# Sums over gathered expert rows: four experts of 32 tokens in column groups in place of one expert of 128 tokens under a diagonal

## The chip, the cores and the metric

The kernel runs on one core of one Trainium2 chip. The metric is the device time of one execution in microseconds (us), the median of several runs.

## The reference

Two transformer blocks run one after the other on 512 tokens of width 1024. The part that the change touches is the last layer of the second block, a retrieval layer over 16384 experts:

```python
query = (ht @ w_query).reshape(t, PEER_HEADS, 2, PEER_HALF)
sub_scores = einsum('thpd,hpkd->thpk', query, sub_keys)
half_vals, half_idx = top_k(sub_scores, 16)
cand = half_vals[:, :, 0, :, None] + half_vals[:, :, 1, None, :]
top_vals, top_pos = top_k(cand, 16)
experts = i1 * 128 + i2                      # from half_idx and top_pos
gates = softmax(top_vals)
u = expert_down[eb]
act = gelu(einsum('td,thkd->thk', xb, u)) * gb
vv = expert_up[eb]
return einsum('thk,thkd->td', act, vv)
```

Each token has 8 heads with 16 experts each; each expert has a down row and an up row of 1024 float32. All arithmetic is in float32.

## The kernel before, in words

There are four tiles of 128 tokens (`TT` = 4, t) and eight heads (`H` = 8), so 32 head steps, n = 8 t + h. Down and up rows lie side by side in one table (`expert_pair_2`), so one indirect DMA fetches for 128 partitions a row of 2048 floats, 1.05 MB. A head step needs 16 of these gathers, and the layer 512. Gather m = 16 n + r brings expert r of each of the 128 tokens, one token to a partition.

The engines run one program each, and meet only at semaphores. For head step n, in eight parts (`PARTS`):

- GpSimd (L822 to L836) waits for the expert numbers (`ids_done`) and for a free buffer (`pair_free`), then issues the gather. There are `PAIRS_0` = 8 buffers during the first eight head steps (`FIRST` = 128 gathers), `PAIRS` = 11 after them (L282 to L303).
- VectorE multiplies the down half with the token row `h2r_2` and sums it (`dot`, L1740 to L1744), two dots to a part, and in parts 2 to 7 does the top-16 selection of head step n + 2 (`topk_part`, L1726); the numbers go to `ids` and the softmax gates to `gate_p` (L1717 to L1724).
- ScalarE (`coefs`, L1207 to L1219) applies Gelu to the dots, multiplies each by its gate (L1214), and writes one 128 x 128 diagonal matrix for each gather, `ident` scaled by the coefficient (L1219). In the first eight head steps it does this for four gathers at a time, later for two.
- TensorE (`up_sums`, L2286 to L2292) multiplies each diagonal with the up half of its buffer, two matmuls of 512 columns in two PSUM banks, and then frees the buffer. A float32 matmul shows as two records in the profile, so a gather has four records on L2290. `edge` (L2302) opens and closes the sums with zero matmuls; `peer_scores` (L2277) makes the scores for the selection.
- After the last head of a tile, `last_norm` (VectorE L1752, ScalarE L1240) adds the result to `xr` and normalizes it; SyncE stores it (L713). It is placed after head step 6 of the next tile.

Tile 0's eight head steps are not alone. The attention of tiles 1 to 3, its output projection and the query projections are cut into 67 steps (`attend(s)`), and a planner (`PLAN`, L573 to L578) deals them by weight over the eight parts of the first six head steps: stick-breaking attention (steps 6 to 28, head steps 0 and 1), forgetting attention, called fox (29 to 56, head steps 2 and 3: L2117 to L2137), then norms, output projection and query projections (57 to 66, head steps 4 and 5); `query_b` goes on to head step 12. In each part every engine does its share of the layer first, then its share of the planned steps. Each engine keeps this order, so a late engine holds up whatever stands behind it in its own program.

The SyncE queue loads weights in an order written out by hand (L693 to L713); among it the loads of `w_query` for head h (L706), each after the projection before it.

The two earlier matmul shapes that matter below: `modulation` (L1798 to L1806) multiplies one or two columns of `cvec` with four different weight slabs, and writes to PSUM partitions 32 j, j = 0 to 3, in a loop over j inside a loop over c.

## Time and profile before

| | us |
|---|---|
| median of 3 runs | 3261.64 |
| lowest, highest | 3260.54, 3271.85 |
| the profiled execution | 3263.08 |
| its span, first to last instruction | 3261.3 |

The page gives for each engine its busy time and for the span in 40 slices of 81.5 us the busy share in tenths. PE is the matmul side of TensorE and PEld its weight loads, which overlap; DVE is VectorE, ACT ScalarE, POOL GpSimd, SP SyncE. PEclk is the clock that was granted to TensorE, as a share of 2.4 GHz: it has two levels, 1.00 (2.4 GHz) and 0.50 (1.2 GHz), and a value between is a mean over time. The DMA row is the busy share of the 16 DMA engines. "Idle before" in a group of instructions is what the engine waited ahead of them, and the arrow names what ended the wait.

### The profile page before, as it was taken

The numbers are of one execution on the slowest core, as the hardware profiler recorded it, in microseconds if no ns is written. First come the engines' busy times: TensorE is split into PE (matmuls) and PEld (weight loads), VectorE is DVE, ScalarE is ACT, GpSimd is POOL, SyncE is SP. The second block draws the span as 40 slices with busy tenths as digits, with TensorE's granted clock in tenths as the row PEclk, the third lists the DMA queues.
The fourth block names the chain that finished last, engine by engine and source line by source line (L and its number), as shares of the span: only waits on it lengthen the run. The fifth ranks groups of instructions, "written<-read, shape, count | busy, mean of one in ns | idle before, by whom it ended". The sixth has DMA issues, their size and how long they took to land.

```text
span 3261.3 us, 27350 instructions
## 1 busy us (share of the span) xinstructions
PE 2663.6 (82%) x8698; PEld 1292.5 (40%) x8698; DVE 1425.1 (44%) x3362; ACT 872.7 (27%) x2245; POOL 661.9 (20%) x601
## 2 busy tenths in 40 slices
PE   2999999956878777399879999889898777777776
PEld 1444554442332333154466545444443332333322
DVE  1295521140000000400157545655667777777774
ACT  2005420011000000211226534232333333333332
POOL 1001100000000000000002111224335455444552
PEclk8999999968888989699789877999999999999998
DMA  7417814728999999512136745689999999999996
GB/s 248 164 52 241 300 61 143 244 95 321 386 377 380 393 387 384 199 65 67 38 128 226 290 163 224 243 317 369 418 417 421 421 421 421 421 398 421 421 421 278
DMA packets 207351, 928.11 MB, mean 285 GB/s; under 512 B 18809, under 2 KB 58808, under 8 KB 124798
## 3 DMA queue, kind: packets, MB, share of 16 engines
q0 software_dynamic: 80704, 558.26, 42.6%
q1 hardware_dynamic: 116736, 359.68, 30.0%
...
## 4 chain that ended last, share of the span: by engine, by line
PE 38%; DMA 20%; DVE 7%; ACT 6%; issue 4%; ACTq 1%; POOL 1%; DVEq 0%; POOLq 0%; SPq 0%
DMA ring<-in_expert_pair,ids 15%; PE bank L2290 9%; PE bank L1995 9%; PE bank L1789 6%; PE bank L2008 4%; PE bank L1795 3%; DMA arena_v<-in_expert_pair,ids 3%; DVE ring L1744 2%; DMA arena_h<-in_expert_pair,ids 1%; ACTq L1002 1%; PE bank L2118 1%; PE bank L2117 1%; ACT arena_h L1219 1%; POOL ring L835 1%; ACT arena_w L1214 1%
## 5 line engine op out<-in xcount | busy, mean ns | idle before, releaser
L2290 PE MATMUL bank<-ring,arena_h 128*128 128x512 f32 x1772 | 840.9, 624 | 183.0 <-ACT arena_h L1219 182.9
L835 POOL DMA_INDIRECT ring<-in_expert_pair,ids x443 | 519.5, 1173 | 1161.3 <-PE bank L2290 633.0
L2290 PEld LDWEIGHTS bank<-ring,arena_h 128*128 128x128 f32 x1772 | 340.0, 198 | 652.6 <-issue 370.2
L1744 DVE CUSTOM_DVE_ANT_0 ring<-ring 128x1024 f32<-128x1024 f32 x315 | 383.8, 1225 | 177.3 <-DMA ring<-in_expert_pair,ids 158.0
L1789 PE MATMUL bank<-arena_h,ring 128*128 128x512 f32 (+1 forms) x1024 | 373.0, 525 | 15.6 <-DMA ring<-in_w_in 13.5
L1995 PE MATMUL bank<-ring,arena_h 128*64 128x512 f32 x1056 | 292.7, 715 | 65.1 <-ACT arena_h L993 62.0
L1789 PEld LDWEIGHTS bank<-arena_h,ring 128*128 128x128 f32 x1024 | 178.7, 196 | 199.1 <-issue 196.1
L1506 DVE TENSOR_TENSOR arena_q<-arena_q,bank 128x256 f32<-128x256 f32 x32 | 13.5, 421 | 528.5 <-ACT arena_q L996 528.5
L1211 ACT ACTIVATE arena_w<-arena_w 128x2 f32<-128x2 f32 (+1 forms) x224 | 45.4, 203 | 627.1 <-DVE arena_w L1744 626.8
L1995 PEld LDWEIGHTS bank<-ring,arena_h 128*64 128x64 f32 x1056 | 103.4, 163 | 229.9 <-issue 195.8
L1744 DVE CUSTOM_DVE_ANT_0 ring<-ring,arena_w 128x1024 f32<-128x1024 f32 x128 | 153.3, 1223 | 68.5 <-DMA ring<-in_expert_pair,ids 64.4
L1219 ACT ACTIVATE arena_h<-ident,arena_w 128x128 f32<-128x128 f32 x512 | 174.1, 393 | 7.3
L2008 PE MATMUL bank<-ring,arena_q 128*64 128x512 f32 x528 | 120.6, 597 | 21.0 <-DVE arena_q L1509 20.5
...
L1795 PE MATMUL bank<-ring,arena_h 128*128 128x512 f32 x224 | 100.9, 610 | 1.0 <-ACT arena_h L1156 0.8
L1347 DVE SCALAR_TENSOR_TENSOR arena_x<-arena_x,convc 128x512 f32<-128x512 f32 x120 | 90.2, 752 | 4.3
L996 ACT ACTIVATE arena_q<-bank 128x256 f32<-128x256 f32 x32 | 12.3, 384 | 287.6 <-PE bank L1995 287.6
L2290 PE MATMUL bank<-arena_v,arena_h 128*128 128x512 f32 x140 | 70.3, 626 | 21.5 <-ACT arena_h L1219 21.5
L1214 ACT ACTIVATE arena_w<-arena_w 128x1 f32<-128x1 f32 x352 | 81.8, 285 | 5.0
L1795 PE MATMUL bank<-ring,arena_q 128*128 128x512 f32 x176 | 78.9, 609 | 3.6 <-DVE arena_q L1406 3.6
L2290 PE MATMUL bank<-arena_h 128*128 128x512 f32 x136 | 66.8, 614 | 17.5 <-ACT arena_h L1219 17.5
L1211 ACT ACT_TABLE_LOAD x49 | 62.9, 1283 | 48.8 <-DVE arena_w L1744 48.2
...
## 6 DMA issues: line engine op xcount, KB each, us to landing
...
ring<-in_w_exp_down SPq DMA_DIRECT2D x33, 2048.0 KB, 13.8
...
arena_h<-xs_d SPq DMA_DIRECT2D x33, 256.0 KB, 13.8
```

The lines of the kernel that those rows point to most:

```text
L835: pool.indirect_dma_start(pair[pair_of(m)], None, A["expert_pair_2"], bass.IndirectOffsetOnAxis(ap=ids[n % 2][:, r:r + 1], axis=0)).then_i ...
L1002: act.dma_start(ys_d[bass.ds(e * CAP, CAP), 512 * half:512 * half + 512], yblk[b][CAP * half:CAP * half + CAP, :]).then_inc(y_dma[b], 16)
L1211: act.activation(gel[:, r0:r0 + count], dots[:, r0:r0 + count], ACT.Gelu).then_inc(gelu_done, 1)
L1214: act.activation(coef[:, r:r + 1], gel[:, r:r + 1], ACT.Copy, scale=gate_p[n % 3][:, r:r + 1]).then_inc(coef_done, 1)
L1219: act.activation(diag[:, r, :], ident[:, :], ACT.Copy, scale=coef[:, r:r + 1]).then_inc(diag_done, 1)
L1347: link(dve.scalar_tensor_tensor(out=conv[:, cc, :], in0=u_pad[:, cc, k:k + T], scalar=convc[:, cc, k:k + 1], in1=conv[:, cc, :], op0=ALU.m ...
L1744: dve.tensor_tensor_reduce(buf, buf, h2r_2[n // H], 1.0, 0.0, ALU.mult, ALU.add, dots[:, r:r + 1]).then_inc(dots_done, 1)
L1789: mm = pe.matmul(dst, w[:, c, at], rhs[:, c, :], start=(c == 0), stop=(c == chunks - 1))
L1795: mm = pe.matmul(dst, xT[:, c, t * P:(t + 1) * P], w[:, c, at], start=(c == 0), stop=(c == chunks - 1))
L1995: mm = pe.matmul(bank[2 + b][at, :].rearrange("p (g f) -> p g f", g=2), xbT[b][:, c, :], gu[:, :, c, 256 * half:256 * half + 256], start=( ...
L2008: mm = pe.matmul(bank[6 + b][CAP * j:CAP * j + CAP, :], hidT[b][:, k, CAP * half:CAP * half + CAP], slab(n)[:, half, k, 512 * j:512 * j + ...
L2290: mm = pe.matmul(bank[4 + 2 * (n // H % 2) + j][:, :], diag[:, r, :], pair[pair_of(m)][:, D + 512 * j:D + 512 * j + 512], start=False, sto ...
```

## The change

Gather m = 16 n + 4 g + j now brings four experts (4 g to 4 g + 3) of the 32 tokens of block j: partition 32 i + q holds expert 4 g + i of token 32 j + q. Four gathers together bring the same rows as before.

- The dots need token block j repeated in the four partition quarters. Sixteen DMAs within SBUF (`load_h2`) copy the 128 token rows of a tile into four such tiles `h2_q`, 2.1 MB written for each tile, from the SyncE queue: for tile 0 before the first dot, for tile t once all dots of tile t - 1 are done. There is one set of `h2_q`. It lies where the diagonals lay and in the second half of ring slot 5, so there is one gather buffer less: 7, then 10. The buffer order after gather 128 begins with the three that come free (`ORDER`), so GpSimd waits for them at m = 128 and no longer at m = 136.
- The numbers and gates must be laid out the same way. `spread` on TensorE does this with 16 matmuls of 32 columns of `ident` and 12 moving columns, VectorE copies the result (`topk_ids`). The selection moves one part earlier, and `spread` and the copy take part 7.
- `gates_at` on VectorE multiplies a 128 x 32 selecting mask with the 16 gates, once for each head step (128 x 512 elements), and ScalarE scales each 128 x 32 matrix by the Gelu result, four gathers at a time throughout. The product with the gate (L1214) is gone.
- `up_sums` runs for four gathers at a time: for each half of the width four matmuls with 32 stationary columns, one to each column group (PSUM partitions 32 j). The buffers are freed by the last four matmuls.
- `peer_scores(n + 2)` and the sums of the last four gathers of head step n - 1 stand at the start of head step n on TensorE; the attention steps keep their places.

```diff
-PAIRS_0, PAIRS = 8, 11
+PAIRS_0, PAIRS = 7, 10
+Q = 32
...
-        diag = view(arena_h, 2048, K16, P)
+        h2_q = [view(arena_h, 2048, D), view(arena_h, 3072, D), ring[:, 5, 2 * D:3 * D], ring[:, 5, 3 * D:4 * D]]
+        sel_q = view(arena_w, 3092, 2, K16, Q)
+        mask_q = sb("mask_q", [P, Q])
...
-        half_i = small(624, 2, K16)
-        id_f = small(656, K16)
+        picked = small(624, 3, K16)
+        half_i = picked[:, 0:2, :]
+        id_f = small(704, K16)
         gsub, gex = small(672, K16), small(688, K16)
-        gate_p = [small(704 + K16 * i, K16) for i in range(2)] + [sb("gate_c", [P, K16])[:, :]]
-        dots, gel, coef = small(736, K16), small(752, K16), small(768, K16)
+        spread_q = [route(4116, 3, K16), route(4164, 3, K16), small(720, 3, K16)]
+        dots, gel = route(4212, K16), route(4228, K16)
...
+        ORDER = list(range(PAIRS_0, PAIRS)) + [(FIRST + k) % PAIRS_0 for k in range(PAIRS_0)]
 
         def pair_of(m):
 
-            return m % PAIRS_0 if m < FIRST else (m - FIRST) % PAIRS
+            return m % PAIRS_0 if m < FIRST else ORDER[(m - FIRST) % PAIRS]
...
+            def load_h2(t):
+
+                for j in range(P // Q):
+                    for i in range(P // Q):
+                        sp.dma_start(h2_q[j][Q * i:Q * i + Q, :], h2r_2[t][Q * j:Q * j + Q, :]).then_inc(h2_q_in, 16)
+
+            sp.wait_ge(h2_done, TT + 1)
+            sp.wait_ge(q_pe, 4)
+            load_h2(0)
...
+                if h == AHEAD + 2:
+                    sp.wait_ge(h2_done, 2 * TT)
+                    sp.wait_ge(dots_done, FIRST)
+                    load_h2(1)
...
+                if t in (1, 2):
+                    sp.wait_ge(dots_done, FIRST * (t + 1))
+                    load_h2(t + 1)
...
-                    if m == PAIRS_0 // 2:
+                    if m == 4:
                         pool.wait_ge(q_pe, 2)
-                    if m == FIRST + PAIRS_0:
+                    if m == FIRST:
...
-            def coefs(n, r0, count):
-
-                m = n * K16 + r0
-                act.wait_ge(dots_done, m + count)
-                act.activation(gel[:, r0:r0 + count], dots[:, r0:r0 + count], ACT.Gelu).then_inc(gelu_done, 1)
-                act.wait_ge(gelu_done, m // count + 1 + (0 if n < H else FIRST // 4 - FIRST // 2))
-                for r in range(r0, r0 + count):
-                    act.activation(coef[:, r:r + 1], gel[:, r:r + 1], ACT.Copy, scale=gate_p[n % 3][:, r:r + 1]).then_inc(coef_done, 1)
-                act.wait_ge(coef_done, m + count)
-                if n > 0:
-                    act.wait_ge(pair_free, m + count - K16)
-                for r in range(r0, r0 + count):
-                    act.activation(diag[:, r, :], ident[:, :], ACT.Copy, scale=coef[:, r:r + 1]).then_inc(diag_done, 1)
-
-            def peer_head(n):
-                for p in range(PARTS):
-                    if p == 0 and n + 2 < TT * H:
-                        queries(n + 2)
-                    if p == 6 and n + 2 < TT * H:
-                        gate_exp(n + 2)
-                    coefs(n, 2 * p, 2)
...
+            def coefs(n, g):
+
+                at = slice(4 * g, 4 * g + 4)
+                act.wait_ge(dots_done, n * K16 + 4 * g + 4)
+                act.activation(gel[:, at], dots[:, at], ACT.Gelu).then_inc(gelu_done, 1)
+                act.wait_ge(gelu_done, 4 * n + g + 1)
+                for k in range(4 * g, 4 * g + 4):
+                    act.activation(sel_q[:, n % 2, k, :], sel_q[:, n % 2, k, :], ACT.Copy, scale=gel[:, k:k + 1]).then_inc(sel_done, 1)
...
+                if part == 5 and n + 2 < TT * H:
                     gate_exp(n + 2)
                 if part % 2 == 1:
-                    coefs(n, 2 * part - 2, 4)
-                    if any(s < ST_FOX for parts in PLAN[n:] for steps in parts for s in steps):
+                    coefs(n, part // 2)
...
+            link(dve.tensor_reduce(mask_q[:, :], ident[:, :].rearrange("p (i q) -> p q i", q=Q), AX, ALU.add))
...
+            def topk_gates(n):
 
                 step = topk_step_of(n, 27)
-                step(dve.scalar_tensor_tensor(out=id_f, in0=half_i[:, 0, :], scalar=float(P), in1=half_i[:, 1, :], op0=ALU.mult, op1=ALU.add))
-                dve.tensor_copy(ids[n % 2][:, :], id_f).then_inc(ids_done, 1)
                 dve.wait_ge(gex_done, n + 1)
                 step(dve.reciprocal(gsum, gsum))
-                step(dve.tensor_scalar(gate_p[n % 3], gex, gsum, None, ALU.mult))
+                step(dve.tensor_scalar(picked[:, 2, :], gex, gsum, None, ALU.mult))
...
+                step = topk_step_of(n, 29)
+                there = bank[0][:, 2 * P:2 * P + 3 * K16].rearrange("p (j c g) -> p c g j", j=4, c=3)
+                dve.wait_ge(spread_pe, n + 1)
+                here = spread_q[n % 3]
+                step(dve.tensor_copy(here.rearrange("p c (g j) -> p c g j", j=4), there))
+                step(dve.scalar_tensor_tensor(out=id_f, in0=here[:, 0, :], scalar=float(P), in1=here[:, 1, :], op0=ALU.mult, op1=ALU.add))
+                dve.tensor_copy(ids[n % 2][:, :], id_f).then_inc(ids_done, 1)
...
-                if part in (2, 3):
-                    topk_half(n, part - 2)
+                if part in (1, 2):
+                    topk_half(n, part - 1)
+                elif part == 3:
+                    topk_sums(n)
                 elif part == 4:
-                    topk_sums(n)
+                    topk_pairs(n)
                 elif part == 5:
-                    topk_pairs(n)
+                    topk_halves_of(n, 0)
                 elif part == 6:
-                    topk_halves_of(n, 0)
+                    topk_halves_of(n, 1)
+                    topk_gates(n)
                 elif part == 7:
-                    topk_halves_of(n, 1)
...
+            def gates_at(n):
+
+                if n >= 2:
+                    dve.wait_ge(pair_free, (n - 1) * K16)
+                link(dve.tensor_tensor(sel_q[:, n % 2, :, :], mask_q[:, :].unsqueeze(1).broadcast_to([P, K16, Q]),
+                                       spread_q[n % 3][:, 2, :].unsqueeze(2).broadcast_to([P, K16, Q]), ALU.mult))
 
             def dot(n, r):
                 m = n * K16 + r
                 dve.wait_ge(pair_in[pair_of(m)], 16 * pair_turn(m))
                 buf = pair[pair_of(m)][:, 0:D]
-                dve.tensor_tensor_reduce(buf, buf, h2r_2[n // H], 1.0, 0.0, ALU.mult, ALU.add, dots[:, r:r + 1]).then_inc(dots_done, 1)
+                dve.tensor_tensor_reduce(buf, buf, h2_q[r % 4], 1.0, 0.0, ALU.mult, ALU.add, dots[:, r:r + 1]).then_inc(dots_done, 1)
 
             def peer_part(n, part):
+                if part == 0:
+                    dve.wait_ge(h2_q_in, 16 * 16 * (n // H + 1))
+                    gates_at(n)
...
-            for part in range(PARTS):
+            for part in range(PARTS - 1):
...
+                    if h == 0 and part == 0:
+                        topk_ids(1)
...
-            def up_sums(n, r):
-                m = n * K16 + r
-                pe.wait_ge(diag_done, m + 1)
-                for j in range(2):
-                    mm = pe.matmul(bank[4 + 2 * (n // H % 2) + j][:, :], diag[:, r, :], pair[pair_of(m)][:, D + 512 * j:D + 512 * j + 512],
-                                   start=False, stop=False)
-                mm.then_inc(pair_free, 1)
+            def spread(n):
+
+                pe.wait_ge(topk_step, 31 * n + 29)
+                for j in range(4):
+                    for i in range(4):
+                        dst = bank[0][Q * i:Q * i + Q, 2 * P + 12 * j:2 * P + 12 * j + 12].rearrange("p (c g) -> p c g", c=3)
+                        mm = pe.matmul(dst, ident[:, Q * j:Q * j + Q], picked[:, :, 4 * i:4 * i + 4], start=True, stop=True)
+                mm.then_inc(spread_pe, 1)
+
+            def up_sums(n, g):
+                m = n * K16 + 4 * g
+                pe.wait_ge(sel_done, m + 4)
+                for half in range(2):
+                    for j in range(4):
+                        mm = pe.matmul(bank[4 + 2 * (n // H % 2) + half][Q * j:Q * j + Q, :], sel_q[:, n % 2, 4 * g + j, :],
+                                       pair[pair_of(m + j)][:, D + 512 * half:D + 512 * half + 512], start=False, stop=False)
+                        if half == 1:
+                            mm.then_inc(pair_free, 1)
 
             def peer_part(n, part):
 
-                if part == 1:
-                    peer_scores(n + 2)
-                if part % 2 == 0 and n + part > 0:
-                    for r in range(4):
-                        up_sums(n if part else n - 1, (2 * part - 4 + r) % K16)
+                if part in (2, 4, 6):
+                    up_sums(n, part // 2 - 1)
+                if part == 7 and n + 2 < TT * H:
+                    spread(n + 2)
...
+                if s == 1:
+                    spread(0)
...
+            for n in range(TT * H):
                 t = n // H
-                if n % H == 0:
+                if n > 0:
+                    if n + 2 < TT * H:
+                        peer_scores(n + 2)
+                    up_sums(n - 1, 3)
+                if n % H == 0 and t > 0:
+                    edge(t - 1, False).then_inc(peer_done, 1)
                     if t >= 2:
                         pe.wait_ge(fin_add, t - 1)
                     edge(t, True)
-                if n + 2 < TT * H:
-                    peer_scores(n + 2)
-                for r in range(K16):
-                    up_sums(n, r)
+                for part in range(PARTS):
+                    peer_part(n, part)
+                    for s in PLAN[n][part] if n < H else ():
+                        attend(s)
+                    if n == 0 and part == 0:
+                        spread(1)
+                        peer_scores(2)
                 if FRONT + AHEAD - 1 <= n + 1 < FRONT + H - 1:
                     query_b(n + 1 - FRONT + 1)
-                if n % H == H - 1:
-                    edge(t, False).then_inc(peer_done, 1)
+            up_sums(TT * H - 1, 3)
+            edge(TT - 1, False).then_inc(peer_done, 1)
```

## Rows read from the trace of the kernel before

**Rows 1.** The page: DMA busy share in 40 slices of 81.5 us.
```profile
DMA  7417814728999999512136745689999999999996
```

**Rows 2.** Busy time by stage: stretch, length, PE, PEld, DVE, ACT, POOL, clock, DMA, GB/s.
```profile
1716.00:1818.00 102.00, 95.61 (x526) 67.97 (x526) 75.79 (x182) 68.81 (x144) 25.36 (x24) 1.00 0.66 248
1818.00:2010.00 192.00, 181.30 (x557) 100.82 (x555) 86.71 (x226) 72.65 (x176) 34.74 (x36) 0.76 0.56 211
2010.00:2120.00 110.00, 96.09 (x248) 46.59 (x248) 71.24 (x152) 40.54 (x90) 24.09 (x24) 0.91 0.65 253
2120.00:2230.00 110.00, 93.39 (x232) 45.47 (x232) 57.51 (x139) 30.73 (x93) 33.80 (x32) 0.93 0.85 324
2230.00:2500.00 270.00, 242.49 (x598) 112.05 (x599) 184.52 (x454) 91.97 (x292) 117.02 (x103) 0.98 1.01 411
2500.00:3200.00 700.00, 534.74 (x1182) 217.35 (x1181) 510.37 (x1233) 251.80 (x784) 351.20 (x276) 0.97 1.01 418
```

**Rows 3.** The chain that ended last, from 2592 us: start, length, what.
```profile
2592.87 20.51 DMA ring<-in_expert_pair,ids
2613.41 1.23 DVE ring L1744
...
2615.88 2.00 PE bank L2290 x4
2617.92 0.76 issue
```

**Rows 4.** TensorE in order of time: L2290 bursts, four gathers each, stick-breaking and fox stage.
```profile
1752.46 7.08 PE L2290 MATMUL bank<-ring,arena_h 128*128 128x512 f32 x16
...
1899.35 8.90 PE L2290 MATMUL bank<-ring,arena_h 128*128 128x512 f32 x16
```

**Rows 5.** Line L1804, weight loads in order of time, 201 to 204 us.
```profile
202.27 0.10 PEld L1804 LDWEIGHTS bank<-ring,cvec 128*1 128x1 f32 x4 [0.33 <-issue]
202.70 0.10 PEld L1804 LDWEIGHTS bank<-ring,cvec 128*1 128x1 f32 x4 [0.33 <-issue]
```

**Rows 6.** Busy time by stage, L2290 alone: PE, PEld, clock, DMA share, GB/s.
```profile
1716.00:1818.00 102.00, 42.66 (x96) 17.76 (x96) 1.00 0.66 248
1818.00:2010.00 192.00, 75.51 (x144) 31.64 (x144) 0.76 0.56 211
2010.00:2120.00 110.00, 46.09 (x96) 19.38 (x96) 0.91 0.65 253
2120.00:2230.00 110.00, 62.03 (x128) 26.10 (x128) 0.93 0.85 324
```

**Rows 7.** VectorE in order of time, a `last_norm`; and the DMA after the next one.
```profile
2554.01 0.69 DVE L1756 TENSOR_TENSOR arena_w<-bank,arena_q 128x512 f32<-128x512 f32 x1
...
2562.28 1.22 DVE L1744 CUSTOM_DVE_ANT_0 ring<-ring 128x1024 f32<-128x1024 f32 x1
...
2850.00:2910.00 60.00, 44.36 (x96) 18.38 (x95) 48.23 (x122) 22.84 (x68) 27.64 (x22) 0.91 0.96 389
```

**Rows 8.** The page's groups: dots, diagonals, gate products.
```profile
L1744 DVE CUSTOM_DVE_ANT_0 ring<-ring 128x1024 f32<-128x1024 f32 x315 | 383.8, 1225 | 177.3 <-DMA ring<-in_expert_pair,ids 158.0
L1219 ACT ACTIVATE arena_h<-ident,arena_w 128x128 f32<-128x128 f32 x512 | 174.1, 393 | 7.3
L1214 ACT ACTIVATE arena_w<-arena_w 128x1 f32<-128x1 f32 x352 | 81.8, 285 | 5.0
```

**Rows 9.** Busy time of L2290 and granted clock, stretches of the fox stage.
```profile
1855.20:1865.50 10.30, 5.26 (x13) 2.04 (x11) 1.00 1.04 411
1865.50:1875.70 10.20, 2.83 (x4) 1.38 (x5) 0.50 0.34 142
```

**Rows 10.** Busy time, all engines, two stretches ahead of the first burst.
```profile
1689.00:1694.80 5.80, 3.28 (x27) 2.90 (x25) 3.90 (x18) 0.00 (x0) 0.00 (x0) 1.00 0.62 258
1694.80:1706.00 11.20, 0.63 (x3) 0.63 (x4) 9.72 (x29) 2.86 (x8) 0.00 (x0) 0.50 0.00 1
```

**Rows 11.** Line L706, the 1 MB loads of w_query from SyncE's queue.
```profile
DMA to landing us min/median/max: 5.7/13.8/26.3
```

33 lines of the change are left out of this document (12 added, 21 removed).

## The prediction

> **What bounds the kernel now.** I read the page first, for the slices: the DMA engines are full from about 2250 us on, and were 10 to 70% busy before that while tile 0's layer ran beside the attention [rows 1]. Then the busy time by stage [rows 2], which shows four stages. In 1716 to 1818 (stick-breaking), 1818 to 2010 (fox) and 2010 to 2230 (output projection, queries) TensorE is busy 95.6 of 102, 181.3 of 192 and 189.5 of 220 us, and the DMA share is 0.66, 0.56 and 0.75 (the mean of 0.65 and 0.85): TensorE sets the pace. From 2230 to 3200 the DMA share is 1.01 and nothing else counts. The chain of waits says the same: in 25 us of it, 20.5 us are a gather on its way, and one turn through dot, diagonals, sums and reissue is the rest [rows 3]. A gather is 1.05 MB, so at the 421 GB/s of a full stretch it costs 2.49 us, four cost 10.0 us, and no change to the engines shortens that. So what counts is how much sooner the kernel leaves the three earlier stages, less what the change adds to the DMA.
>
> **TensorE's sums.** Four gathers now are 16 records in 7.08 us at the full clock, 0.43 us each, and 8.90 us where a burst starts at the low clock [rows 4]. Afterwards they are 16 records too, but to four column groups in turn. `modulation` already has this pattern, with four different moving tensors: its weight loads go out in fours every 0.43 us [rows 5], so four records share the time of one. I take 4 x 0.43 = 1.73 us for four gathers at the full clock, 3.5 us at half of it. Its stationary tiles are one column wide and not 32, so the bound on the other side is no overlap at all, 7.08 us.
> The Trainium skill (TensorE: Matmul & The Clock Gate, Measured speedup vs the span model) gives 2.38x for three column groups, not 3x; scaled alike a burst would take about 2.2 us, an estimate from that page, which adds some 10 us over the three stages. The same skill (TensorEngine Tiling (Array Packing), Key Properties) says that changing the tiling mode drains TensorE, which speaks against short bursts between attention matmuls; no row here prices such a drain apart.
>
> **Stick-breaking, 102 us, 6 bursts.** L2290 has 42.7 us [rows 6]; 6 x 1.73 = 10.4 replace it, and one and a half `spread` add about 3 (32 records; at least 1 us, four at a time every 0.1, at most 6, at 0.19 each as a weight load of [rows 6]). TensorE's 95.6 falls to 66. Next is VectorE with 75.8, plus 0.9 us a head step for `gates_at` and the copy (a 512-element operation takes 0.69 [rows 7]). ScalarE drops: four diagonals and gate products are 4 x (0.393 + 0.285) = 2.7 us of durations, four scalings lie between 4 x 0.285 and 4 x 0.393, say 1.3 [rows 8]. The floor is 78 us; the engines wait for each other step by step, so I take 88: **-14** (between -24 and 0).
>
> **Fox, 192 us, 9 bursts.** L2290 has 75.5 us, everything else on TensorE 105.8 [rows 2, 6]. 144 records at 0.43 would be 62, so 13 us more is 31 records at the low clock, 27 us in all. The stage's mean clock 0.76 means 92 us low and 100 high; less the bursts and 11 us idle, the attention matmuls ran some 60 us at the low and 46 at the high level. The clock rises inside a burst and falls about 5 us after it [rows 9]; the fox matmuls, with 64 or 8 rows and short moving parts, do not hold it. With bursts of 3.5 us it may not rise at all. All low: 60 + 2 x 46 + 9 x 3.5 + 11 = 194 us, no gain. All high: 30 + 46 + 16 = 92, where VectorE (86.7 plus waits) and the DMA (0.56 x 192 = 107) take over, about 110 us. Not every record doubles at the low clock, and the first part still has stick-breaking steps; I take 170, near the low end, since [rows 9] is nearest to it: **-22** (between -82 and +2).
> The Trainium skill (TensorE: Matmul & The Clock Gate, What's actually happening) has the same direction, that the throttled clock is the default and activity releases it; the clock in [rows 9] agrees.
>
> **Output projection and queries, 220 us, 14 bursts.** L2290 has 108.1 us [rows 6]; 14 x 1.9 = 27 replace it. TensorE falls to 108, VectorE has 129, the DMA 165 (0.65 x 110 + 0.85 x 110) [rows 2]. With 7 buffers freed four at a time, three gathers (7.5 us) are on their way when the last of a group lands, and the turn back is 1.23 (dot, [rows 8]), up to 2.5 (selection; VectorE's 510 of 700 us [rows 2] are 29 us a head step of 40, less 16 dots 9.5 over six parts, 1.6 on the mean), 0.3 and 1.3 (ScalarE), 1.7 to 2 (sums), 0.8 (wake-up, [rows 3]), about 1 for the issue: 8 to 9.5 us. So one or two us of every ten are lost, and 165 becomes 195: **-25** (between -50 and 0). One buffer less is priced here.
>
> **Start.** `load_h2(0)` lands while the first eight gathers sit in full buffers (DMA share 0.00 from 1694.8 to 1706, [rows 10]): nothing. `spread(0)` and its copy stand before the first gather: **+2** (1 to 6).
>
> **The reloads of `h2_q`.** Tiles 1 to 3 each add 2.1 MB in a stretch where the DMA is full: 3 x 5.0 = **+15**. They also hold VectorE: 16 issues on SyncE's queue and a landing beside gathers; 1 MB from this queue took 5.7 to 26 us [rows 11]. Behind that wait stand all dots of the tile, then ScalarE, TensorE and GpSimd. The cover: six gathers under way and four reissued, 25 us, plus the 5 us of the load itself; the first new group is free 8 to 10 us after the load lands. So a landing in 17 us or less costs nothing more, one in 27 costs 10 each: 15 to 45 us. In SyncE's queue only a `w_query` load is behind it, needed a head step later.
>
> **The full stretch otherwise.** With 10 buffers, six gathers (14.9 us) cover a turn of 8 to 9.5 us. The sums of four no longer queue on TensorE. `last_norm` holds VectorE 8.3 us, and after the second one the DMA already fell to 0.96 over 60 us, 3 us [rows 7]. With 5 to 6 us of slack in place of a longer queue, I expect 2 to 3 us at each of three: **+4** net (0 to 12). GpSimd's earlier wait at m = 128 is met, since queries of head 1 are projected in head step 5. At the end the last four sums are about 1 us shorter: **-1**.
>
> **Sum.** -14 - 22 - 25 + 2 + 15 + 4 - 1 = -41. The profiled execution took 3263.1 us, 1.4 above the median of the runs; 3263.1 - 41 = 3222, and against the median 3221.
>
> **The rivals.**
> - *The cover was thicker than I think*: the clock stays high in the fox stage and each stage reaches its next floor: -24 - 80 - 45 + 20 = -129, 3133 us. For it: the DMA is idle for over 200 us in these stages. Against it: the clock in [rows 9]. Chance 0.12.
> - *The gain goes no further than the start*: fox at the low clock throughout (0), stick-breaking -7, output -12 since the norm chain and 7 buffers bind, against +20: about 3262 us. For it: VectorE and ScalarE have chains in every step. Chance 0.15.
> - *The clock falls in stick-breaking too* (slower): the attention matmuls there, 52.9 us, all at the high level now, would take 106, and bursts 21, so the stage takes 132 in place of 102; with fox +2, output -10 and +20: 3304 us. It decides when TensorE is too idle between bursts. Against it: at 57% busy the clock was still high, and low only after a stretch at 6% [rows 10]; after the change it is about 75% busy here. Chance 0.07.
> - *Groups of four starve the DMA in the full stretch*: it begins where the turn exceeds 14.9 us. At 17 us it costs 2 us for each of 96 groups, about 3400 us. Chance 0.04.
> - *The change doesn't do what it says*: column groups with 32 stationary columns do not overlap. The stages stay, the additions remain: 3280 us. [rows 5] speaks against it. Chance 0.04.
>
> **How the numbers follow.** My forecast has 0.58. About 0.5% (16 us) is what a measurement of this kernel can tell from no change. Faster: 0.58 + 0.12 = 0.70; same: 0.15; slower: 0.07 + 0.04 + 0.04 = 0.15. The range runs from 3165, where half of the fox bound is reached, to 3285, which takes in the second rival, the fifth and the dear reloads.
>
> **What would show it.** The sums' bursts in fours every 0.43 or 0.85 us; TensorE under 80% busy in stick-breaking and VectorE next; the clock mostly 0.50 in the fox stage with a stage of about 170 us; the full stretch beginning 60 us earlier and the DMA at 421 GB/s in it, with three SBUF loads of 5 us each; VectorE waiting 10 to 17 us at three tile changes. I am wrong if the fox stage shortens by over 40 us or not at all, if DMA gaps open at the tile changes, or if the DMA share in the full stretch falls below 0.97.

## The result, and the profile after

The changed kernel takes 3342.8 us (median of four runs, 3331.9 to 3356.7) where the kernel before, on the same chip, takes 3261.1: a ratio of 1.0246 with a 95% interval of 1.0201 to 1.029. It is slower by 2.5%; the forecast was 3221 us, 1.2% faster.

The page of the kernel after: totals, busy slices of TensorE and VectorE, granted clock, DMA share and rate (slices of 83 us), and the group of the new sums.

```profile
span 3330.2 us, 28788 instructions
PE 2163.6 (65%) x9722; PEld 992.1 (30%) x9722; DVE 1452.2 (44%) x3427; ACT 682.5 (20%) x1636; POOL 610.6 (18%) x601
PE   2998999948878878499777867545543343333433
DVE  1385520140000000401267556554667577747775
PEclk8998999958888888689788778767666665665656
DMA  7417815638999997521146765789999899999997
GB/s 245 158 51 244 296 50 158 221 127 341 387 381 378 385 381 289 205 76 51 51 161 246 287 255 216 277 318 337 404 404 421 315 419 421 417 355 367 421 421 314
L2333 PE MATMUL bank<-ring,arena_w 128*32 128x512 f32 x1736 | 419.7, 960 | 521.6 <-ACT arena_w L1236 521.6
```

The DMA row is full from about the same place as before [rows 1], but its rate does not stay at 421 GB/s: it falls to 315 in one later slice and to 355 and 367 in two, where tiles change. The stages, busy time by engine, to be held against [rows 2] (columns as there):

```profile
1717.00:1849.00 132.00, 93.11 (x732) 75.82 (x732) 98.95 (x230) 70.33 (x139) 26.96 (x28) 0.84 0.55 212
1849.00:2003.00 154.00, 120.29 (x596) 62.99 (x597) 89.94 (x222) 64.92 (x142) 30.46 (x33) 0.76 0.69 269
2003.00:2250.00 247.00, 139.01 (x620) 57.86 (x619) 139.94 (x330) 52.55 (x129) 68.10 (x64) 0.74 0.73 277
2284.00:3200.00 916.00, 371.38 (x2244) 104.92 (x2244) 648.90 (x1584) 176.46 (x543) 371.84 (x334) 0.62 0.98 393
```

TensorE did get its relief: it was 94% busy in the first two stages, and is now 71 and 78% busy, and 41% in the long stretch. The time did not follow. A burst of sums for four gathers, in order of time, in the fox stage, and behind it one from the stick-breaking stage:

```profile
1885.85 0.95 ACT L1236 ACTIVATE arena_w<-arena_w 128x32 f32<-128x32 f32 x4
1886.85 0.20 PEld L2333 LDWEIGHTS bank<-ring,arena_w 128*32 128x32 f32 x8 [0.75 <-ACT arena_w L1236]
1886.85 3.19 PE L2333 MATMUL bank<-ring,arena_w 128*32 128x512 f32 x16 [0.57 <-ACT arena_w L1236]
1887.71 0.20 PEld L2333 LDWEIGHTS bank<-ring,arena_w 128*32 128x32 f32 x4 [0.66 <-issue]
1888.56 0.20 PEld L2333 LDWEIGHTS bank<-ring,arena_w 128*32 128x32 f32 x4 [0.66 <-issue]
```
```profile
1733.08 1.92 PE L2333 MATMUL bank<-ring,arena_w 128*32 128x512 f32 x16 [1.55 <-ACT arena_w L1236]
```

Sixteen records in 3.19 us, where [rows 4] has 8.90, in fours every 0.85 us; and in 1.92 us, where it has 7.08. The column groups share their time, as forecast. And a tile change: the chain that ended last (start, length, what), the wait for the copies from the table of waits (us in all, times, longest), and busy times across it.

```profile
2615.64 1.23 DVE ring L1772
...
2616.90 0.59 SPq L703
...
2626.44 0.59 SPq L703
...
2627.07 21.47 DMA ring<-ring
...
2648.57 0.70 DVE arena_w L1765
```
```profile
DVE arena_w L1765 <- DMA ring<-ring: 94.1, 3, 31.7
```
```profile
2605.00:2615.00 10.00, 4.08 (x48) 0.94 (x48) 8.84 (x18) 2.75 (x8) 4.52 (x5) 0.66 1.01 422
2615.00:2627.00 12.00, 8.41 (x28) 2.98 (x28) 1.97 (x5) 1.47 (x6) 5.59 (x6) 0.72 1.03 361
2627.00:2637.00 10.00, 0.00 (x0) 0.00 (x0) 0.00 (x0) 0.00 (x0) 1.46 (x2) 0.66 1.03 288
2637.00:2648.60 11.60, 0.00 (x0) 0.00 (x0) 0.03 (x1) 0.00 (x0) 0.00 (x0) 0.50 1.01 292
2648.60:2660.00 11.40, 3.64 (x16) 0.60 (x16) 10.24 (x26) 1.16 (x5) 0.33 (x1) 0.50 0.34 141
2660.00:2670.00 10.00, 3.37 (x16) 0.60 (x16) 8.60 (x23) 2.44 (x6) 4.37 (x5) 0.62 0.87 338
```

After the last dot of tile 1 SyncE issues the sixteen copies, 0.59 us each (one 1.26), and for twenty us nothing but the DMA and two issues on GpSimd is at work: VectorE waits for the rows, 94.1 us at the three changes, 31.7 at the longest. While they land the DMA engines are busy, but move 290 GB/s in place of 421. Then the buffers are full and unread, and the DMA is idle most of the next 11 us. Over the 55 us from 2615 to 2670 the answers add up to 15.6 MB where 421 GB/s would be 23.2: 7.6 MB, 18 us, are missing, about half before the landing and half after, and 2.1 MB more, 5 us, were the copies' own.

**Where the time went.** For a comparison free of what lies ahead of the layer I take the start of a fixed dot in each trace, counted from the 5000th TensorE record, which lies in code that both kernels share. That record came at 1660.1 us in the profile of before and at 1670.4 after; over all kernels below it lies between 1657.5 and 1676.0, and both ends belong to variants of the changed kernel whose code up to there is the same. So some 10 of the 69 us between the two profiles stand ahead of the layer, and one trace can't tell how many of them are chance. The table has the us from that record to dot 0, dots 0 to 32 (stick-breaking), 32 to 64 (fox), 64 to 127 (output projection and queries), 127 to 511 (tiles 1 to 3), and 511 to the end; it serves for the experiments too.

| kernel | start | 0-32 | 32-64 | 64-127 | 127-511 | rest | median |
|---|---|---|---|---|---|---|---|
| before | 42.5 | 128.4 | 194.6 | 226.2 | 990.3 | 19.2 | 3261-3270 |
| after | 46.6 | 131.8 | 153.7 | 247.9 | 1060.2 | 19.5 | 3342.8 |
| a_again | 46.4 | 132.2 | 163.8 | 250.0 | 1058.7 | 20.9 | 3344.8 |
| a_noreload | 46.4 | 131.9 | 164.4 | 247.1 | 993.9 | 20.5 | 3280.3 |
| a_pe_rep | 46.3 | 132.7 | 163.0 | 248.1 | 1028.2 | 19.8 | 3314.7 |
| a_rep_early | 41.8 | 133.7 | 163.5 | 247.2 | 1006.4 | 19.2 | 3279.4 |
| a_dram | 41.8 | 134.8 | 161.9 | 251.5 | 1124.0 | 20.1 | 3406.4 |
| b_7_10 | 42.6 | 131.7 | 195.0 | 250.1 | 988.2 | 19.2 | 3294.4 |
| n_8_11 | 41.8 | 126.2 | 145.8 | 224.4 | 987.4 | 20.4 | 3222.9 |
| a_pairs | 41.8 | 121.6 | 153.5 | 211.9 | 1060.8 | 19.3 | 3277.9 |
| b_pairs | 42.6 | 121.6 | 160.0 | 205.9 | 989.0 | 19.2 | 3206.5 |
| c_pe | 41.8 | 121.4 | 153.5 | 209.5 | 1003.5 | 19.7 | 3217.7 |
| c_pe_all | 41.8 | 121.5 | 153.5 | 212.8 | 996.4 | 17.2 | 3207.1 |
| n_8_11_pairs | 41.8 | 121.6 | 153.5 | 195.2 | 987.4 | 19.9 | 3193.0 |

Each row is one trace. `after` and `a_again` are the same kernel, and their fox stages differ by 10 us (153.7 and 163.8); a difference of that size in this column is not shown by a single trace.

Two losses stand against one gain: +68 to +70 us in tiles 1 to 3, +22 to +24 in the output and query stage, -31 to -41 in the fox stage.

### The profile page after: what moved, and what is told of

The parts are those of the page before. It is cut to its first block, busy times and chain, and to the rows that moved or that the text cites. A ratio compares the mean times of both kernels' runs of the same rounds, so it can differ in the third digit from the quotient of the medians.

```text
span 3330.2 us, 28788 instructions
## 1 busy us (share of the span) xinstructions
PE 2163.6 (65%) x9722; PEld 992.1 (30%) x9722; DVE 1452.2 (44%) x3427; ACT 682.5 (20%) x1636; POOL 610.6 (18%) x601
## 3 DMA queue, kind: packets, MB, share of 16 engines
q0 software_dynamic: 80704, 558.26, 42.5%
## 4 chain that ended last, share of the span: by engine, by line
PE 34%; DMA 18%; DVE 11%; ACT 6%; issue 6%; ACTq 1%; POOL 1%; SPq 1%; another core or an unknown queue 0%; DVEq 0%; POOLq 0%
DMA ring<-in_expert_pair,ids 13%; PE bank L2028 9%; PE bank L1822 7%; PE bank L2333 6%; DVE ring L1772 4%; PE bank L2041 4%; PE bank L1828 3%; DMA arena_v<-in_expert_pair,ids 3%; DMA ring<-ring 2%; ACT arena_w L1236 1%; ACTq L1024 1%; SPq L703 1%; PE bank L2316 1%; POOL ring L857 1%; ACT arena_h L1015 1%
## 5 line engine op out<-in xcount | busy, mean ns | idle before, releaser
L2333 PE MATMUL bank<-ring,arena_w 128*32 128x512 f32 x1736 | 419.7, 960 | 521.6 <-ACT arena_w L1236 521.6
L857 POOL DMA_INDIRECT ring<-in_expert_pair,ids x434 | 468.3, 1079 | 1286.3 <-PE bank L2333 839.0
L1822 PE MATMUL bank<-arena_h,ring 128*128 128x512 f32 (+1 forms) x1024 | 372.3, 524 | 15.9 <-DMA ring<-in_w_in 13.8
L1772 DVE CUSTOM_DVE_ANT_0 ring<-ring 128x1024 f32<-128x1024 f32 x217 | 264.4, 1225 | 177.6 <-DMA ring<-in_expert_pair,ids 167.5
L2333 PEld LDWEIGHTS bank<-ring,arena_w 128*32 128x32 f32 x1736 | 72.0, 150 | 760.4 <-ACT arena_w L1236 622.6
L1772 DVE CUSTOM_DVE_ANT_0 ring<-ring,arena_h 128x1024 f32<-128x1024 f32 x217 | 263.1, 1226 | 79.9 <-DMA ring<-in_expert_pair,ids 67.5
L1517 DVE TENSOR_TENSOR arena_q<-arena_q,bank 128x256 f32<-128x256 f32 x32 | 13.5, 421 | 535.1 <-ACT arena_q L1018 535.1
L2333 PE MATMUL bank<-arena_h,arena_w 128*32 128x512 f32 x156 | 132.7, 1003 | 76.2 <-ACT arena_w L1236 76.2
L2333 PE MATMUL bank<-arena_v,arena_w 128*32 128x512 f32 x156 | 133.2, 1006 | 0.0
L1236 ACT ACTIVATE arena_w<-arena_w 128x32 f32<-128x32 f32 x512 | 122.4, 309 | 4.2
L1828 PE MATMUL bank<-ring,arena_h 128*128 128x512 f32 x224 | 100.8, 610 | 1.0 <-ACT arena_h L1178 0.8
L1822 PE MATMUL bank<-arena_q,ring 128*128 128x384 f32 x224 | 82.7, 532 | 0.0
## 6 DMA issues: line engine op xcount, KB each, us to landing
ring<-in_w_exp_up SPq DMA_DIRECT2D x33, 2048.0 KB, 12.4
```

The lines of the kernel that those rows point to most:

```text
L857: pool.indirect_dma_start(pair[pair_of(m)], None, A["expert_pair_2"], bass.IndirectOffsetOnAxis(ap=ids[n % 2][:, r:r + 1], axis=0)).then_i ...
L1236: act.activation(sel_q[:, n % 2, k, :], sel_q[:, n % 2, k, :], ACT.Copy, scale=gel[:, k:k + 1]).then_inc(sel_done, 1)
L1772: dve.tensor_tensor_reduce(buf, buf, h2_q[r % 4], 1.0, 0.0, ALU.mult, ALU.add, dots[:, r:r + 1]).then_inc(dots_done, 1)
L1822: mm = pe.matmul(dst, w[:, c, at], rhs[:, c, :], start=(c == 0), stop=(c == chunks - 1))
L1828: mm = pe.matmul(dst, xT[:, c, t * P:(t + 1) * P], w[:, c, at], start=(c == 0), stop=(c == chunks - 1))
L2333: mm = pe.matmul(bank[4 + 2 * (n // H % 2) + half][Q * j:Q * j + Q, :], sel_q[:, n % 2, 4 * g + j, :], pair[pair_of(m + j)][:, D + 512 * h ...
```

## The experiments

All are timed against the kernel before on their own chip; a ratio is to that. The levels of before in the four sets of runs were 3266 to 3270 us.

### The tile change

**a_again**: no edit.

> The changed kernel once more, as the level for the others. In its first profile the same code ahead of the layer ended 10.4 us later than in the kernel before. Theory 'prelude is chance': here that offset is within 3 us of nothing and the ratio to the kernel before is 1.020 to 1.025, because the four times of the first look already spread over 25 us. Rival 'prelude belongs to the changed kernel' (its 32-row mask, its layout): the offset is 8 to 12 us again.

3344.8 us, ratio 1.0226 (1.0199 to 1.0252). The loss repeats. The shared code ended 11.6 us later than in the profile of before, which is what the rival expected. All traces together leave it open: the eleven of the changed kernel and its variants lie between -2.6 and +15.9 us, 9 on average, the two other kernels with diagonals at 9.7 (b_7_10) and -0.6 (b_pairs). A spread of 18 us with the same code is chance; whether a few us ahead of the layer belong to the change, these traces can't tell.

**a_noreload**: the three reloads are left out, so tiles 1 to 3 use the rows of tile 0.

```diff
-                if h == AHEAD + 2:
-                    sp.wait_ge(h2_done, 2 * TT)
-                    sp.wait_ge(dots_done, FIRST)
-                    load_h2(1)
...
-                if t in (1, 2):
-                    sp.wait_ge(dots_done, FIRST * (t + 1))
-                    load_h2(t + 1)
...
-                    dve.wait_ge(h2_q_in, 16 * 16 * (n // H + 1))
+                    dve.wait_ge(h2_q_in, 16 * 16)
```

> Leaves out the three reloads of the spread token rows at the tile changes (the dots of tiles 1 to 3 are taken with the rows of tile 0), everything else as in the changed kernel. Theory A (the loss is the tile change: landing about 31 us after the first of 16 issues, 9 to 12 of it recovered, three times): 60 to 70 us less than the changed kernel, dots 128, 256 and 384 without their jumps, DMA share over 0.97 across the tile changes. Rival B (ten buffers released in fours starve the gathers of the full stretch): less than 20 us less. Rival C (the loss is all ahead of the full stretch): under 5 us less.

3280.3 us, ratio 1.0023 (1.0002 to 1.0043): 64.5 us less than a_again, and in the table dots 127 to 511 take 993.9 in place of 1058.7, the other stages the same within 3 us. The reloads are 64.8 of the 68.4 us lost behind tile 0, 21.6 us each; ten buffers and groups of four cost the long stretch 3.6 us against before, no more. Theory A holds, B and C fall.

**a_pe_rep**: TensorE spreads the rows, between the old tile's last sums and the opening of the new ones.

```diff
+            def replicate(t):
+                for j in range(4):
+                    if j > 0:
+                        pe.wait_ge(rep_act, 4 * (t - 1) + j)
+                        pe.wait_ge(rep_dve, 4 * (t - 1) + j)
+                    for half in range(2):
+                        for i in range(4):
+                            mm = pe.matmul(bank[4 + 2 * (t % 2) + half][Q * i:Q * i + Q, :], ident[:, Q * j:Q * j + Q],
+                                           h2r_2[t][:, 512 * half:512 * half + 512], start=True, stop=True)
+                    mm.then_inc(rep_pe, 1)
...
+                    replicate(t)
                     edge(t, True)
```

> The rows of a new tile are spread by TensorE (identity columns as the stationary operand, 32 matmuls of 128x32 by 512 in four rounds, copied out of PSUM by ScalarE and VectorE) and by no DMA. At half clock a round is two overlapped groups of 0.92 us or so and a copy of 0.6 to 0.8, so four rounds take 8 to 12 us, behind the 4 us of the last up rows; ten buffers hold 25 us of gathers. Theory A: 50 to 68 us less than the changed kernel, DMA share over 0.95 across the changes, gathers not waiting. Rival A2 (at a tile change the gathers need the VectorE and TensorE time, whoever spreads the rows): 25 to 40 us less, with 8 to 12 us of idle DMA at each change. Rivals B and C: less than 20 us less.

3314.7 us, ratio 1.0132 (1.0105 to 1.0159): 30 us less, rival A2's size. In order of time, from the last dots of tile 1, and the DMA behind it:

```profile
2628.53 2.13 PE L2363 MATMUL bank<-zeros 128*128 128x512 f32 x4
2630.59 1.92 PE L2376 MATMUL bank<-ring,ident 128*32 128x512 f32 x16
2632.93 0.69 DVE L1771 COPY arena_h<-bank 128x512 f32<-128x512 f32 x1 [10.25 <-PE bank L2376]
2633.77 1.92 PE L2376 MATMUL bank<-ring,ident 128*32 128x512 f32 x16 [1.26 <-DVE arena_h L1771]
2641.59 0.69 DVE L1771 COPY ring<-bank 128x512 f32<-128x512 f32 x1 [2.20 <-PE bank L2376]
```
```profile
2630.50:2632.60 2.10, 2.01 (x17) 0.42 (x16) 0.00 (x0) 0.00 (x0) 1.66 (x2) 1.00 1.02 425
2637.00:2643.00 6.00, 4.07 (x34) 1.17 (x27) 2.06 (x3) 1.19 (x2) 0.00 (x0) 1.00 1.01 419
2643.00:2648.00 5.00, 1.39 (x4) 0.32 (x2) 4.89 (x10) 0.19 (x1) 0.00 (x0) 1.00 0.19 77
2648.00:2654.00 6.00, 3.42 (x16) 0.58 (x16) 4.87 (x17) 0.98 (x5) 0.74 (x1) 0.72 0.00 0
```

The gathers run at full rate while TensorE works, so nothing is lost to slower DMA. But the four rounds take 2.9 us each and start only after the last sums and the closing of the old tile: VectorE is away for some 20 us, and ten buffers do not cover 20 plus a turn: 10 us of idle DMA, as rival A2 said.

**a_rep_early**: the same, the first three rounds ahead of the last sums; block j is copied out once the dot that last reads it is done.

```diff
+                if turns(n) and part == 6:
+                    replicate(n // H + 1, 0)
...
+                if turns(n) and part == 7:
+                    replicate(n // H + 1, 1)
+                    replicate(n // H + 1, 2)
...
+                    if turns(n - 1):
+                        replicate(t, 3)
                     up_sums(n - 1, 3)
```

> The rows of a new tile spread by TensorE as in the first such run (3314.7 us), but begun before the old tile's last dots: block j is copied out as soon as the dot that last reads its rows is done, and the last block goes ahead of the last up rows. The wait of VectorE at a change should fall from 19.6 us to 4 to 8 and the 10 us in which no gather ran should go. Theory A (at a tile change only the time until the rows are there counts): 25 to 34 us less than that run, 3281 to 3290 us, the level of the run without reloads. Rival (the burst order at the change costs the gathers whatever is done): under 15 us less.

3279.4 us, ratio 1.0039 (1.0014 to 1.0063), 35 us less again, and with that the level of a_noreload. By the table 22 of the 35 are in dots 127 to 511; the others stand at the start and ahead of the layer, where this edit changes nothing. At the second change the DMA no longer stops:

```profile
2608.00:2618.00 10.00, 7.49 (x68) 2.25 (x60) 5.06 (x11) 3.37 (x9) 2.42 (x2) 1.00 1.01 420
2618.00:2628.00 10.00, 5.72 (x28) 1.85 (x24) 9.07 (x23) 1.16 (x5) 6.23 (x5) 1.00 0.99 391
```

What is left of the cost, 12 us of dots 127 to 511, lies nearly all in the first change: there a query projection (10.6 us) stands between the third round and the fourth in TensorE's program, and VectorE waits 15.8 us for the fourth.

```profile
2257.27 10.59 PE L1848 MATMUL bank<-arena_q,ring 128*128 128x384 f32 x32
2273.92 0.69 DVE L1790 COPY ring<-bank 128x512 f32<-128x512 f32 x1 [15.82 <-PE bank L2373]
```

**a_dram**: the reload from a DRAM copy, four DMAs whose source repeats 32 rows four times.

```diff
+                for j in range(P // Q):
+                    sp.dma_start(h2_q[j], h2_d[t - 1, Q * j:Q * j + Q, :].unsqueeze(0).broadcast_to([P // Q, Q, D])).then_inc(h2_q_in, 16)
```

> The changed kernel with the reloads of tiles 1 to 3 read from a copy of the rows in DRAM, in 4 DMAs of 128 partitions each in place of 16 of 32 partitions (the copies are written in the output and query stage, 1.5 MB, 4 us of DMA). If the landing is slow because 16 issues of 0.6 us and 32-partition transfers between SBUF partitions stand in front: VectorE waits 14 to 20 us in place of 31.7, and the time is 30 to 50 us less than the changed kernel. If the 2 MB share the DMA engines with the ten queued gathers and land behind them whatever their form: 22 to 32 us of wait, under 20 us less.

3406.4 us, ratio 1.0423 (1.0373 to 1.0473): both expectations failed, it is 62 us slower than the changed kernel. VectorE's wait and the stretch with nothing but these loads on the way:

```profile
DVE arena_w L1775 <- DMA ring<-h_d: 155.0, 3, 53.0
2680.00:2700.00 20.00, 0.00 (x0) 0.00 (x0) 0.00 (x0) 0.00 (x0) 0.00 (x0) 0.50 0.29 111
```

With the gathers stopped the loads move 100 to 120 GB/s at a busy share of 0.25 to 0.32, about what four of sixteen engines would show. The source pattern has an outermost dimension of four. The Trainium skill (DMA: Bandwidth & Descriptors, Rules for kernel authors) says that an outermost dimension smaller than 16 limits how many engines a DMA uses, and that a leading zero-stride broadcast of c copies confines it to at most c engines; the share of 0.25 agrees. So this run prices that form, and whether fewer, larger issues would land sooner stays open.

### The stages beside the attention

**b_7_10**: the kernel before with one buffer less.

```diff
-PAIRS_0, PAIRS = 8, 11
+PAIRS_0, PAIRS = 7, 10
...
+        ORDER = list(range(PAIRS_0, PAIRS)) + [(FIRST + k) % PAIRS_0 for k in range(PAIRS_0)]
...
-            return m % PAIRS_0 if m < FIRST else (m - FIRST) % PAIRS
+            return m % PAIRS_0 if m < FIRST else ORDER[(m - FIRST) % PAIRS]
```

> The kernel before with 7 and 10 gather buffers in place of 8 and 11, nothing else changed. Theory D (the lost buffer is what the output and query stage pays, +22 us there against a forecast of -25): dot 128 comes 10 to 25 us later than in the kernel before, and 256, 384 and 511 no later than that beyond 5 us more; time 3270 to 3290 us. Rival E (release in fours is what costs there, a buffer alone little): dot 128 within 5 us, time within 8 us of the kernel before.

3294.4 us, ratio 1.0074 (1.0049 to 1.0099). The output and query stage takes 250.1 us, 24 more than before, which is what the changed kernel takes (247.9, 250.0) with far less of TensorE's work in it: TensorE is busy 139 of 247 us there, and 203 of 250 in b_7_10. Stick-breaking +3, the same as in the changed kernel; fox and the long stretch nothing. The loss is a little more than theory D gave it (dot 128 comes 28 us later against 10 to 25, and the time is 4 us over its window), and it is where theory D put it: with seven buffers that stage has its pace from the buffers, and TensorE's relief is worth nothing in it.

**n_8_11**: the changed kernel with the buffers of before, without the three reloads and without half of the first load (the `load_h2` lines, not shown).

```diff
-PAIRS_0, PAIRS = 7, 10
+PAIRS_0, PAIRS = 8, 11
...
-        h2_q = [view(arena_h, 2048, D), view(arena_h, 3072, D), ring[:, 5, 2 * D:3 * D], ring[:, 5, 3 * D:4 * D]]
+        h2_q = [view(arena_h, 2048, D), view(arena_h, 3072, D), view(arena_h, 2048, D), view(arena_h, 3072, D)]
```

> As the run without the three reloads (its level 3280 us), and with the gather buffers of the kernel before, 8 and 11: the room comes from letting token blocks 2 and 3 share the spread rows of blocks 0 and 1, so that only half of the first load is left and the dots of two groups in four are taken with other rows. Theory D (TensorE's gain in the first tile was there, and the missing buffer ate it): 18 to 30 us less than the run without reloads, nearly all of it between dots 64 and 127, the time 3250 to 3262 us, faster than the kernel before. Rival E (the release in fours and the slow clock hold the output and query stage, whatever the buffers): within 8 us of 3280.

3222.9 us, ratio 0.9868 (0.9821 to 0.9916), 57 us less than a_noreload, twice what theory D gave the buffer. The output stage gives 23 us back, to 224.4, and that is before's 226.2: even with eight buffers TensorE's relief bought nothing there while the sums went in fours. The fox stage falls to 145.8, stick-breaking by 6 and the long stretch by 6. So the expectation that nearly all of it lies in the output stage failed: a buffer that was worth nothing in fox with diagonals (b_7_10) is worth 18 us there against a_noreload, or 8 against the faster of the two traces of the changed kernel.

**a_pairs**: the changed kernel with the first tile in pairs.

```diff
+                if part % 2 == 0 and n < H:
+                    coefs_of(n, part // 2, 0, 2)
...
+                if n < H and part % 2 == 1:
+                    up_sums(n, part // 2, 0, 2)
                 if part in (2, 4, 6):
-                    up_sums(n, part // 2 - 1)
+                    up_sums(n, part // 2 - 1, 2 if n < H else 0)
```

> The changed kernel with the gathered rows of the first tile weighted, summed and released in pairs, not in fours (two column groups at a time, so a pair takes TensorE as long as a four did). If the release in fours is what costs in the output and query stage: dot 127 comes 8 to 20 us earlier than in the changed kernel, the gain after dot 64. If TensorE's doubled time for the up rows costs more than the earlier release gives: dot 48 comes 10 to 25 us later, and dot 127 is not earlier. The jumps at the tile changes stay.

3277.9 us, ratio 1.0026 (1.0006 to 1.0047): 67 us less than the changed kernel, though a pair uses two of the four column groups and so a row takes twice TensorE's time. That is three times what was expected, and not only behind dot 64: against a_again tile 0 gains 11, 10 and 38 us (the 10 of the fox stage are within the spread of its traces). How a group of four held the buffers shows on GpSimd in the changed kernel, output stage, the gathers in order of time with the idle time before each:

```profile
2150.38 0.94 POOL L857 DMA_INDIRECT ring<-in_expert_pair,ids  x1 [8.69 <-PE bank L2333]
2151.62 1.60 POOL L857 DMA_INDIRECT ring<-in_expert_pair,ids  x1 [0.30 <-issue]
2153.53 0.94 POOL L857 DMA_INDIRECT ring<-in_expert_pair,ids  x1 [0.30 <-issue]
2154.77 0.94 POOL L857 DMA_INDIRECT ring<-in_expert_pair,ids  x1 [0.30 <-issue]
2162.85 0.93 POOL L857 DMA_INDIRECT ring<-in_expert_pair,ids  x1 [7.14 <-PE bank L2333]
2164.09 0.93 POOL L857 DMA_INDIRECT ring<-in_expert_pair,ids  x1 [0.30 <-issue]
```

Four gathers leave together, 12.5 us after the four before them: 3.1 us a row, and the DMA needs 2.49. (Other groups are up to 24 us apart, so the stage's mean is 3.9.) A buffer's turn is the time from the issue of a gather into it to the issue of the next. Averaged over dots 64 to 119, from the starts of dots and of gathers in the traces:

| kernel | buffers | issue to dot | dot to reissue of its buffer | turn | turn / buffers |
|---|---|---|---|---|---|
| before | 8 | 12.0 | 19.6 | 31.6 | 3.95 |
| b_7_10 | 7 | 10.8 | 19.6 | 30.3 | 4.33 |
| a_again | 7 | 11.2 | 18.3 | 29.5 | 4.21 |
| n_8_11 | 8 | 12.6 | 17.4 | 30.0 | 3.75 |
| a_pairs | 7 | 13.4 | 12.4 | 25.8 | 3.68 |
| b_pairs | 8 | 13.1 | 16.4 | 29.5 | 3.69 |

With fours a buffer stays 17 to 20 us after its dot: the programs make a group's first two dots wait a part for the next two, and the sums stand another part behind, after that part's attention step. The last column is the pace at which gathers are issued in this stretch; from dot to dot the stage runs 0.2 to 0.4 us a row faster.

**b_pairs**: the kernel before, diagonals and all, with the first tile in pairs.

```diff
-                if part % 2 == 1:
-                    coefs(n, 2 * part - 2, 4)
-                    if any(s < ST_FOX for parts in PLAN[n:] for steps in parts for s in steps):
-                        act.preload_act_table_set(EXP_LN)
+                coefs(n, 2 * part, 2)
+                if any(s < ST_FOX for parts in PLAN[n:] for steps in parts for s in steps):
+                    act.preload_act_table_set(EXP_LN)
...
-                if part % 2 == 0 and n + part > 0:
-                    for r in range(4):
-                        up_sums(n if part else n - 1, (2 * part - 4 + r) % K16)
+                if n + part > 0:
+                    for r in range(2):
+                        up_sums(n if part else n - 1, (2 * part - 2 + r) % K16)
```

> The kernel before, diagonals and 8 and 11 buffers, with coefficients and up rows of the first tile taken in pairs in place of fours, each row still released by its own two matmuls. If the hold of a buffer after its dot is what sets the first tile's pace in any of these kernels: dot 127 comes 20 to 50 us earlier than in the kernel before, and the gain is not one of column groups. If in the kernel before TensorE (2.2 us a row at half clock, 80 to 93% busy to the end of the fox stage) holds the stick and fox stages: dot 64 within 10 us of before, 5 to 20 us gained behind it.

3206.5 us, ratio 0.9817 (0.9789 to 0.9846): with no TensorE work removed, the kernel before gains 62 us in tile 0, more than the 20 to 50 expected, and 35 of them in the fox stage that TensorE was thought to bound; there the second expectation (dot 64 within 10 us of before) failed. The waits of the fox stage, before (1831 to 2025 us) and with pairs (1824 to 1984): waits in us, times, longest; and the busy times (columns as in [rows 2]).

```profile
POOL ring L835 <- PE bank L2290: 118.6, 31, 20.7
DVE smx L1598 <- PE bank L2119: 81.6, 19, 13.2
1831.00:2025.00 194.00, 178.43 (x524) 96.64 (x524) 86.62 (x217) 72.40 (x172) 34.82 (x37) 0.76 0.61 233
```
```profile
POOL ring L835 <- PE bank L2289: 96.1, 26, 10.4
DVE smx L1597 <- PE bank L2118: 49.2, 23, 8.1
1824.00:1984.00 160.00, 146.72 (x531) 78.34 (x530) 87.34 (x218) 98.69 (x202) 36.25 (x36) 0.93 0.76 281
```

VectorE's softmax waits for score matmuls that stand in TensorE's program behind a burst of sums. A burst of four gathers, 7 to 9 us, holds up the chain of the attention; a burst of two holds it half as long, and the clock is 0.93 where it was 0.76 [rows 2]. In this stage it is the burst and not the number of buffers: with one buffer less b_7_10 took the same 195 us. TensorE's share of the stage did not fall: 178 of 194 us before, 147 of 160 here, both 92%, with the same work. Which share of the gain is order and which is clock no run here separates.

### Both repairs, and what is left for the column groups

**c_pe** (a_rep_early with pairs in tile 0: both edits above) and **c_pe_all** (`n < H` dropped from them: pairs in all tiles).

> Both repairs together: rows of a new tile spread by TensorE before the old tile's last dots, and the gathered rows of the first tile weighted, summed and released in pairs. Theory F (the two losses are separate: a buffer of the first tile is held too long, 18 to 20 us from its dot to its reissue in place of 12, and the reload at the tile changes): the gains add up, 67 + 65 us less than the changed kernel less a few, so 3212 to 3225 us, 1.2 to 1.7% faster than the kernel before; dot 127 about 529 us behind the end of the code ahead of the layer, dots 127 to 511 in 1003 to 1009 us. Rival (they share a cause, and the later stage gives back what the first tile gains, as a full DMA stretch moved to earlier would not): over 3240 us.

> As c_pe, with pairs in all four tiles. If the hold of a buffer matters only where buffers are few (7 against 10): within 4 us of c_pe, and DMA share of the full stretch as before, 1.0, since ten buffers cover a hold of 25 us at 2.5 us a row. If the release in fours also costs the full stretch (last_norm, tile changes): 5 to 15 us less. If the doubled TensorE time or the further table loads on ScalarE get in the way: 5 us or more slower.

c_pe: 3217.7 us, ratio 0.9852 (0.9827 to 0.9877). Theory F: the two losses are separate and their repairs add up (127 us of 132). It is 1.5% faster than the kernel before. c_pe_all: 3207.1, ratio 0.9831 (0.9798 to 0.9864); its 127 to 511 is 7 us shorter and the rest 2.5, its 64 to 127 3 us longer. That fits the second expectation, but the intervals overlap.

**n_8_11_pairs**: n_8_11 and pairs.

> Column groups with 8 and 11 buffers and no later reloads (the run n_8_11, 3223 us, again with half of the first load and the three others left out), and pairs in the first tile: what the change could be worth against diagonals (b_pairs, 3206.5 us) with buffers and hold alike. If TensorE's own time still sets the fox stage once the hold is short: dots 32 to 64 in 135 to 150 us (160.0 with diagonals), and the time 3180 to 3198 us. If the hold was all there was to gain: dots 32 to 64 in 153 to 162 us, and the time 3198 to 3212 us, no faster than diagonals in pairs.

3193.0 us, ratio 0.9776 (0.9747 to 0.9806). The time is in the first window, the fox stage (153.5) in the second. Against diagonals in pairs, with as many buffers (though in the output stage a buffer is held 13.1 us after its dot here and 16.4 there), the column groups gain nothing in stick-breaking, 6 us in fox and 11 in the output stage, 13.5 between the medians; the two ratios' intervals overlap, and this kernel leaves out all reloads. The relief was real but came at a lower clock:

```profile
1831.00:1985.00 154.00, 133.51 (x594) 65.17 (x595) 89.94 (x223) 87.04 (x166) 34.77 (x35) 0.81 0.75 285
```

TensorE is busy 134 us at 0.81 here, and 147 us at 0.93 in b_pairs. What the column groups would be worth in this stage at an equal clock no run shows. With the reloads as cheap as c_pe has them, and a buffer less, they at best draw level: 3207 and 3218 against b_pairs' 3206.5. By the table c_pe gains 3 us in tile 0 against b_pairs and loses 14.5 in dots 127 to 511.

## Why the prediction was wrong, point by point

- **Where the kernel is bound.** The step that failed first: "TensorE sets the pace". Shares of 94% in stick-breaking and fox were read as a bound. b_pairs takes no work from TensorE and shortens the three stages by 7, 35 and 20 us; the column groups, with fours and eight buffers (n_8_11), leave the output stage as it was. A part of the 181 busy us was work at half the clock, and VectorE's chain was waiting behind long bursts. The share itself could not tell: with pairs it is as high (92% in fox), in a stage 35 us shorter.
- **TensorE's sums**: right. A burst wholly at half clock takes 3.64 us against 3.5 forecast, one at the full clock 1.92 against 1.73. That is 3.7 times under the 7.08 of [rows 4]. The Trainium skill (TensorE: Matmul & The Clock Gate, Measured speedup vs the span model) has 2.38x for three column groups; scaled to four, an estimate from that page, this is 3.2x, less than was measured here. (The prediction's "some 10 us" for it is 14: 29 bursts at 0.5 us.)
- **Stick-breaking, -14**: measured +3.5. TensorE fell to 93 of 132 us and VectorE, at 99, was far from its floor. Buffers and their hold set the pace: b_7_10 loses the same 3 us, and pairs gain 10. With pairs it is 121.6 us with diagonals or column groups, seven buffers or eight; what bounds it then is open. The clock fell to 0.84, so the rival on it was half right, but its 30 us did not come. The ground given against it was misread: in [rows 10] the clock is low from the start of the stretch at 6%, and not only after it.
- **Fox, -22**: measured -41 and, again, -31. The size is near, the reason mostly not TensorE's work: shorter bursts give -35 without removing any, and the column groups give 6 on top of them. The clock did not fall as feared: 0.76 and 0.71, against 0.76 before.
- **Output and queries, -25**: measured +22 to +24, the second large error. "One buffer less is priced here" was the step: a turn back of 8 to 9.5 us was summed from the durations of dot, selection, scaling and sums. From the dot to the reissue it measured 18.3, since the engines' programs put a part with its attention step between each two of them. The DMA's 165 us was no floor that this stage could come near.
- **Start, +2**: +4 in four traces, -0.7 in the seven others of the changed kernel, which is outside 1 to 6. No edit accounts for the difference.
- **The reloads, +15 (15 to 45)**: measured +65, the largest error. The step that failed is the landing: the sum took 17 us or less, the range at most 27, and it took 31.7, of which 10.2 are the sixteen issues one after the other. The rule "a landing in 17 us or less costs nothing more, one in 27 costs 10 each" was near: for 31.7 us it gives 19.7 with the copies' own 5. And copies beside gathers were priced by their bytes: they also slowed all traffic to 290 GB/s. At the second change 23 us are lost by the bytes counted above; a_noreload says 21.6 for each. The prediction named gaps at the tile changes as a sign that it is wrong; they came.
- **Full stretch, +4**: a_noreload has +3.6. Right. **End, -1**: +0.3 to +1.7.

The sum by the table, a_again against before: 3.9 + 3.8 - 30.8 + 23.8 + 68.4 + 1.7 = 70.8, and 11.6 ahead of the layer; the two medians on that chip are 75.5 apart.
